# Turning attention probabilities as 64-query halves in one run, in a one-core decoder layer

## The reference

```python
s = jnp.einsum('bqhd,bkhd->bhqk', qb, kb).astype(jnp.float32) * scale   # keys 0 .. end of this block
p = jax.nn.softmax(jnp.where(mask, s, NEG_INF), axis=-1)
outs.append(jnp.einsum('bhqk,bkhd->bqhd', p, vb))
```

## Time and profile before

| | us |
|---|---|
| median of 3 runs (1407.98 to 1408.33) | 1408.01 |
| the profiled execution | 1408.35 |
| its span | 1406.6 |
| PE busy in the span | 1396.8 (99%) |
| DVE busy | 1038.2 (74%) |
| ACT busy | 684.6 (49%) |
| POOL busy | 165.4 (12%) |

### The profile page before, as it was taken

One profiled execution on the slowest core, in us unless ns is written; L12 is line 12 of the kernel. 1 busy time (PEld: TensorE's weight loads), 2 busy tenths in 40 slices (PEclk: granted clock), 3 DMA queues, 4 the chain that ended last, 5 costly groups with the idle time before them and its releaser, 6 DMA issues.

```text
span 1406.6 us, 19078 instructions
## 1 busy us (share of the span) xinstructions
PE 1396.8 (99%) x6986; PEld 1166.7 (83%) x6986; DVE 1038.2 (74%) x1527; ACT 684.6 (49%) x1111; POOL 165.4 (12%) x174
## 2 busy tenths in 40 slices
PE   9999999999999999999999999999999999999999
PEld 7988888888788888878888888888888888888887
DVE  6888666656876657769545888778877777588886
ACT  6344356656555431266323755555555555434332
POOL 2002511103361021123000100000000000000000
PEclk9999999999999999999999999999999999999999
DMA  7022211241121223277622222222222224890222
GB/s 266 30 84 69 76 53 61 66 136 38 55 61 40 83 76 91 77 247 253 239 92 75 60 90 90 72 78 90 90 75 90 87 64 147 316 386 4 97 75 82
DMA packets 131111, 149.99 MB, mean 107 GB/s; under 512 B 11402, under 2 KB 93245, under 8 KB 130621
## 3 DMA queue, kind: packets, MB, share of 16 engines
q1 hardware_dynamic: 130832, 148.72, 32.1%
q10 hardware_dynamic: 189, 0.08, 0.0%
HBM read 111.88 MB, written 36.31 MB: 105 GB/s over the span
## 4 chain that ended last, share of the span: by engine, by line
PE 97%; DVE 1%; ACT 1%; DMA 1%; issue 0%; SPq 0%; POOL 0%; ACTq 0%
PE ps L2566 30%; PE ps L945 18%; PE ps L2875 5%; PE ps L2876 5%; PE ps L2877 5%; PE ps L2966 4%; PE ps L1152 3%; PE ps L3528 2%; PE ps L3530 2%; PE ps L3529 2%; PE ps L1129 2%; PE ps L482 2%; PE ps L484 2%; PE ps L483 2%; PE ps L1848 2%; PE ps L443 1%
## 5 line engine op out<-in xcount | busy, mean ns | idle before, releaser
L2566 PE MATMUL ps<-split_arena 128*128 128x512 f32 x1320 | 306.4, 389 | 0.8 <-ACT up_part L2451 0.8
L2566 PEld LDWEIGHTS ps<-split_arena 128*128 128x128 f32 x1320 | 247.6, 188 | 52.6 <-issue 1.2
L945 PE MATMUL ps<-split_arena 128*128 128x512 f32 x1152 | 290.3, 399 | 0.5 <-ACT plain_arena L980 0.4
L945 PEld LDWEIGHTS ps<-split_arena 128*128 128x128 f32 x1152 | 208.6, 188 | 41.5 <-issue 1.5
L2749 ACT ACTIVATE down_ops<-down_all 128x1024 fp32r<-128x1024 f32 x77 | 81.5, 1061 | 114.9 <-PE ps L2877 112.9
L2768 DVE TENSOR_TENSOR down_ops<-down_all,down_ops 128x1024 fp32r<-128x1024 f32 x77 | 94.0, 1221 | 45.7 <-ACT down_ops L2749 45.6
L2566 PE MATMUL ps<-up_b,split_arena 128*128 128x512 f32 x528 | 127.0, 389 | 0.0
L2875 PE MATMUL ps<-down_ops 128*128 128x512 f32 x308 | 119.9, 389 | 0.0
L2876 PE MATMUL ps<-down_ops 128*128 128x512 f32 x308 | 119.8, 389 | 0.0
L2877 PE MATMUL ps<-down_ops 128*128 128x512 f32 x308 | 119.8, 389 | 0.0
L2566 PEld LDWEIGHTS ps<-up_b,split_arena 128*128 128x128 f32 x528 | 99.0, 188 | 20.5
(11 more groups left out here) (452 smaller groups left out, 2598.3 us busy)
## 6 DMA issues: line engine op xcount, KB each, us to landing
plain_arena<-in_w_in SPq DMA_DIRECT2D x26, 512.0 KB, 4.0
scr_gate<-plain_arena SPq DMA_DIRECT2D x48, 256.0 KB, 2.0
plain_arena<-scr_gate SPq DMA_DIRECT2D x24, 512.0 KB, 4.5
plain_arena<-in_w_up SPq DMA_DIRECT2D x22, 512.0 KB, 5.2
up_raw<-in_w_up SPq DMA_DIRECT2D x22, 512.0 KB, 4.8
scr_act<-plain_arena SPq DMA_DIRECT2D x22, 512.0 KB, 2.6
down_all<-scr_act SPq DMA_DIRECT2D x18, 512.0 KB, 9.7
down_all<-in_w_down SPq DMA_DIRECT2D x18, 512.0 KB, 10.8
```

The lines of the kernel that those rows point to most:

```text
L945: mm = nc.tensor.matmul(m.ps[:, self.banks[half], :], w[:, k, :], src[:, k, h * BANK:(h + 1) * BANK], start=(j == 0), stop=(j == self.PER_ ...
L2566: mm = nc.tensor.matmul(o, self.w[j][w][:, k, :], self.h[j][k][h], start=(j in self.OPENS and k == 0 and n == 0), stop=(k == self.HK - 1 a ...
```

## The change

A query tile with five to eight key tiles still gives two fills, but fill e holds all its key tiles for queries 64e to 64e + 63, and both are turned in one run: for each key tile a transpose of the rows 0 to 63 into one bank and one of the rows 64 to 127 into the other. The run waits for the lo part of fill f - 1, so that both banks are free. In steps that also turn a qk fill, `behind` now stands between the qk fill and the run; in the other steps with two fills it stands after the run. The second `turn` (fox) loses its column offset in the same way as the first.

```diff
-            fills += [("p", s, a, min(4, s % TT + 1 - a)) for a in range(0, s % TT + 1, 4)]
+            fills += [("p", s, e, s % TT + 1) for e in range(2 if self.in_halves(s) else 1)]
...
+    @staticmethod
+    def in_halves(s):
+        return s % TT >= 4
+
+    def turn_halves(self, pe, f):
+        _, s, _, n = self.fills[f]
+        pe.wait_ge(self.lo, f)
+        for j in range(n):
+            for e in range(2):
+                r, bank = slice(64 * e, 64 * e + 64), 4 + (f + e) % 2
+                tr = self.m.nc.tensor.transpose(self.m.ps[:, bank, 64 * j:64 * j + 64], self.p_buf[s % 2][r, j * P:(j + 1) * P], self.m.ident[r, r])
+                if j == n - 1:
+                    tr.then_inc(self.turned, 1)
...
-            for f in self.qk_fills(s):
+            moving = self.qk_fills(s)
+            for f in moving:
                 self.turn(pe, f)
+            if moving and self.in_halves(s):
+                self.fill.tensor(pe, behind)
             pe.wait_ge(self.normed, s + 1)
-            *first, last = self.fills_of("p", s)
-            for f in first:
-                self.turn(pe, f)
-
-            if first:
-                self.fill.tensor(pe, behind)
-            self.turn(pe, last)
-            if not first:
+            first, *second = self.fills_of("p", s)
+            if second:
+                self.turn_halves(pe, first)
+            else:
+                self.turn(pe, first)
+            if not (moving and self.in_halves(s)):
                 self.fill.tensor(pe, behind)
...
-            _, s, a, n = x
-            slot = self.kept_at(s % TT)
-            return [self.pt[e][:, a:a + n, slot, :] for e in range(2)], self.m.ps[:, 4 + f % 2, 0:n * P].rearrange("p (j q) -> p j q", q=P)
+            _, s, e, n = x
+            slot, q = self.kept_at(s % TT), P // 2 if self.in_halves(s) else P
+            return [p[:, 0:n, slot, q * e:q * e + q] for p in self.pt], self.m.ps[:, 4 + f % 2, 0:n * q].rearrange("p (j q) -> p j q", q=q)
...
-            for f in self.qk_fills(s):
+            moving = self.qk_fills(s)
+            for f in moving:
                 self.split_hi(act, f)
-            *first, last = self.fills_of("p", s)
-            for f in first:
-                self.split_hi(act, f)
-            if first:
+            if moving and self.in_halves(s):
                 self.fill.scalar(act, behind)
                 self.fill.copy_made(act)
-            self.split_hi(act, last)
-            if not first:
+            for f in self.fills_of("p", s):
+                self.split_hi(act, f)
+            if not (moving and self.in_halves(s)):
                 self.fill.scalar(act, behind)
```

More of the change, by code:

```diff
@@ L1103, in turn @@
         if x[0] == "p":
-            _, s, a, n = x
+            _, s, _, n = x
             for j in range(n):
-                tr = nc.tensor.transpose(bank[:, j * P:(j + 1) * P], self.p_buf[s % 2][:, (a + j) * P:(a + j + 1) * P], m.ident[:])
+                tr = nc.tensor.transpose(bank[:, j * P:(j + 1) * P], self.p_buf[s % 2][:, j * P:(j + 1) * P], m.ident[:])
         else:
```

## The result

| | before | after |
|---|---|---|
| median, us | 1408.07 | 1422.28 |
| lowest and highest | 1407.98, 1408.33 | 1421.81, 1423.17 |
| profiled execution | 1408.35 | 1423.17 |
| its span | 1406.6 | 1421.5 |

The ratio is 1.0102 (95% interval 1.009 to 1.0113): 14.2 us slower. The forecast was 1418.2 us within 1411 to 1424, slower with 0.87. The sign was right, and so was the mechanism in the main (TensorE waits for lo parts that come late); the size was 10.2 us where 14.2 came, and one term and one stage had another cause than forecast.

A forecast was written before the change was run, and what follows sets the result against it. The prediction took TensorE, busy for 99% of the span, as the bound. Terms 1.5 + 3.2 + 4.6 + 2.0 - 0.9 - 0.2 = +10.2 us on 1408.35, with the median 0.34 lower, gave 1418.2 us, 8-in-10 range 1411 to 1424.

The forecast's parts named there:

- The array: TensorE's time for the transposes themselves: half pairs 0.067 us apart, but dear ends; +0.05 us per head, 0.4 in all.
- rivals 2: Half pairs run fast, mode change hidden or absent, gain not lost again: 8.9 us less, 1399 us; chance 0.05.
- 3 (no pairing): Halves follow each other instead of running side by side: 9 us more, 1427 us; chance 0.04.
- rival 1: New waits turn out covered by slack in DVE's order; +0.4 us less the last heads' gain, 1408 us; chance 0.09.
- Rival 4: GpSimd's gate splits and DVE's norm slow each other, or the exponential comes late: half as much again, 1424 us; chance 0.14.
- the runs of 64 elements: ACT and DVE writing in runs of 64 and not 128: bounded at 0 to 1.4 us, taken as 0.
- i = 5: Step of later heads: halves wait for the qk fill's lo part; +1.5 us over six heads, less 0.2 absorbed in MLA.
- i = 7 to i = 0: Seam between heads: the next head's single transpose waits for the halves' lo part; +0.77 us each, six seams, +4.6 us.
- i = 4: Halves wait for the lo part of the preceding step's fill, written by DVE behind the norm; together +2.0 us.
- i = 6: Halves wait for the qk fill's lo part: +0.5, +0.84, +0.24 us in first, second, third head; +3.2 us for two attentions.
- Last heads: No qk fills; transposes together give ACT time for the gate copy, so waits go: about -0.45 us each, -0.9 us.
- all other stages unchanged: Outside the two attentions, the latent stage included, no stage was expected to change: 0 us.

The follow-up runs named there:

- e2_full: The changed kernel's order and waits, but with full 128x128 transposes in two fills of key tiles, turned in one run: 1421.99 us.
- e3_seam: The changed kernel with six gate products put between the next head's scores and its first transpose, in the second to fourth head: 1415.24 us.
- e7_last: The kernel before with full transposes; in the last head of both attentions only, both fills together, `behind` after them, `copy_made` behind the last step: 1406.37 us.
- e1_copy: The changed kernel with ACT again copying a finished gate half out right behind the last step's products, in both attentions: 1420.2 us.
- e4_switch: The kernel before with one more 64-row transpose ahead of each second fill of probabilities, 32 in all: 1418.37 us.

## Why the prediction was right, and where it was off

**The array.** Right. The halves run as the S5 rows said: in the seam above 16 halves take 0.71 - 0.22 = 0.49 us from first to last start, 0.07 per pair, 0.32 us behind the last product. TensorE's busy time rose by 0.8 us where I had 0.4, and e2_full shows the exchange to be even within the scatter. In half-height pairs a run of 5 to 8 key tiles neither pays nor costs here; rivals 2 (faster) and 3 (no pairing) are excluded, as is rival 1 by e3_seam. Rival 4 (late work spreads) named 1424, nearer to the result than my 1418.2, but its mechanism is not there: POOL, DVE and ACT are busy for 165.7, 1037.6 and 683.5 us where they were for 165.4, 1038.2 and 684.6, and the steps that I counted as free got no later. The same busy times say that the runs of 64 elements cost nothing, as I had taken it.

**i = 5.** Right, 1.5 us for 1.3 to 1.5: halves released by the lo part of the qk fill. In the changed kernel, MLA's third head (beside rows 5):
```profile
461.93 0.60 PE L1131 MATMUL ps<-ident,plain_arena 128*96 128x128 f32 x4
462.13 1.23 DVE L1314 CUSTOM_DVE_ANT_0 ps<-ps,mla_mask 128x1024 f32<-128x1024 f32 x1 [1.43 <-PE ps L1145]
...
463.28 0.75 DVE L1329 SCALAR_TENSOR_TENSOR split_arena<-ps,colv,split_arena 96x512 fp32r<-96x512 f32 x1
...
464.18 0.59 PE L1082 MATMUL ps<-ident,plain_arena 64*128 64x64 f32 x12 [0.27 <-DVE split_arena L1329]
464.69 2.34 PE L945 MATMUL ps<-split_arena 128*128 128x512 f32 x9
```
The lo part ends 2.10 us after the qk fill, as before; the halves start at +2.25 (I had +2.15).

**i = 7 to i = 0.** Right place, too small a size, 4.6 for 6.3 us, the largest error among the waits. Last product at 440.01 + 1.07 - 0.39 = 440.69, single transpose at 443.22: +2.53, where I had +2.40. The product behind it follows 0.12 us later; where the transpose had not waited it was 0.03. I had taken 0.05 us from the end of a lo part to the transpose, which is what rows 6 show: but there a weight load was waiting. Here the weights are in place and the transpose itself waits for its bank, and it comes 0.15 us after the write, as in the rows above (lo part to 464.03, halves at 464.18). The 24 waits of this kind in the attentions of the changed kernel all ended 0.144 to 0.148 us after the write. The load of the next product's weights, too, starts only 0.09 us behind the transpose, where it started with it in rows 7. A wait thus costs some 0.2 us beyond the difference of the two times, and there are six of these; the rest is that the products came 0.41 us earlier and not 0.44. That i = 4 has 2.4 for 2.0 us for the same reason fits, but is not worked out.

**i = 6.** Right in sum, 2.8 for 3.2, but by luck: the cause is another. I had the halves wait for the lo part of the qk fill, by 0.5, 0.84 and 0.24 us in the first, second and third head. No halves waited in i = 6. In the changed kernel, MLA's third head, whose qk fill starts at 466.87:
```profile
467.07 0.60 ACT L980 ACTIVATE plain_arena<-ps 128x512 f32<-128x512 f32 x1 [0.34 <-PE ps L945]
...
467.81 1.60 PE L945 MATMUL ps<-split_arena 128*128 128x512 f32 x6 [0.34 <-ACT plain_arena L980]
...
468.27 0.75 DVE L1329 SCALAR_TENSOR_TENSOR mla_kt<-ps,colv,mla_kt 96x512 fp32r<-96x512 f32 x1 [1.93 <-ACT mla_kt L1236]
...
469.35 0.65 PE L1082 MATMUL ps<-ident,plain_arena 64*128 64x64 f32 x14
```
The products, now directly behind the qk fill, wait for the gate copy to empty their bank; that is the 2.2 us of L980, 0.34 to 0.41 in each of the six heads. The lo part ends at 469.02, well before the halves at 469.35. ACT is not late either: the copy ends 0.80 us after the qk fill, as in the kernel before. I had computed the copy's end and not asked who else waits for it.

**Last heads.** Right: -0.9, and e7_last shows that this gain needs no halves.

**The latent stage.** The step that failed is "all other stages unchanged". By medians it is 2.1 us (e1_copy) of the 4.1 that are missing; in the profiled execution, the slowest of the four, 2.5. The diff takes a `copy_made` out of ACT's last step; I had followed ACT's orders only for steps in which another exponential comes next, which empties the bank anyway, and there is none after the last. e1_copy shows it. Most of the rest that is missing is the seams, 1.7 us.

## What to carry to other kernels

Before one makes an engine's run shorter, look at what that run covers and what it hands on in parts: here the first half of the transposes both hid a wait and let ACT and DVE begin, and doing all in one run lost both. When queues are ordered by hand, follow each removed line to the end of its loop, in every queue behind it; the costliest wait that I missed was a load that stood behind a store that waited for a copy. And counts of filler work are tied to the buffers that they fill, not only to the time that they cover.

## What the runs showed of the hardware

The rows of the kernel before showed the price of a switch only in S5. e4_switch shows that a single 64-row transpose between full-height work costs 0.32 us on the average of 32, though a half in S5's stream takes 0.03. This agrees with the Trainium skill ("TensorEngine Tiling (Array Packing)", Key Properties: a change of tiling mode drains the engine); no trace here shows the drain itself. A pair side by side goes at 0.07 us against 0.11 for a full one; with what going in and out costs in rows 4, a run needs about seven key tiles to be even, an estimate from rows 3 and 4.

A wait for a semaphore does not cost the same everywhere: a weight load started 0.05 us after the end of the write that released it (rows 6: 247.71, 247.76), a matrix product whose weights were loaded and whose bank was not free 0.15 us after it (464.03, 464.18), whether DVE or ACT had released it.
